# Products whose results nobody reads, in the gaps of TensorE, in a two-block fp32 kernel on one core

## What is computed

```
def reference(x, positions, ..., ffn_w1_2, ffn_w2_2, gla_..., ssd_...):
    x = first_block(x, positions, ...)
    return second_block(x, c_2, ctx_2, c_ctx_2, ...)

# second_block, per layer i in (0, 1); 256 latent and 256 context tokens
ul = snake(modulate(hl, m_l[0], m_l[1]));  uc = modulate(hc, m_c[0], m_c[1])
yc, yl = gla_mixer(uc, ul, ...)  if i == 0  else  ssd_mixer(uc, ul, ...)
hl = layer_norm(ALPHA * hl + m_l[2] * snake(yl))
hl = layer_norm(ALPHA * hl + m_l[5] * sq_relu_mlp(modulate(hl, m_l[3], m_l[4]), ffn_w1[i], ffn_w2[i]))
```

## Time and profile before

| what | value |
|---|---|
| median of 3 runs | 2241.13 us (2236.27 to 2246.55) |
| the profiled execution | 2240.53 us, span 2238.3 us |
| TensorE busy | 2014.4 us, 90% of the span |
| DVE, ACT, POOL busy | 1229.2, 729.5, 167.2 us |
| mean granted clock of TensorE | 0.961 |

### The profile page before, as it was taken

The page is one execution under the profiler, slowest core; times in us unless marked ns, Lnnn a source line. Parts: engine busy times, 40 slices in busy tenths (PEclk is TensorE's granted clock), DMA queues, the critical chain, the costliest instruction groups (busy, mean ns, idle before and its releaser), DMA issues.

```text
span 2238.3 us, 30881 instructions
## 1 busy us (share of the span) xinstructions
PE 2014.4 (90%) x12070; PEld 1447.9 (65%) x12070; DVE 1229.2 (55%) x2175; ACT 729.5 (33%) x1316; POOL 167.2 (7%) x155
## 2 busy tenths in 40 slices
PE   7989889879998778969998999999989988998997
PEld 4776433327785323326886788888867776777896
DVE  3474411134473212147466686666667876877676
ACT  3452201014552101124324311121165437654332
POOL 2001100001002000015422100000100000000000
PEclk9999999989998999988999999999999998999999
DMA  7589699975597899952221332232222342324552
GB/s 237 179 287 337 262 409 405 371 300 177 197 364 260 333 393 402 364 193 76 76 76 76 107 119 102 87 113 76 84 76 90 109 151 94 132 108 165 198 188 95
DMA packets 151921, 440.23 MB, mean 197 GB/s; under 512 B 10369, under 2 KB 12849, under 8 KB 143457
## 3 DMA queue, kind: packets, MB, share of 16 engines
q1 hardware_dynamic: 142704, 412.72, 49.3%
q0 software_dynamic: 8352, 22.39, 3.5%
q10 hardware_dynamic: 720, 3.15, 0.3%
HBM read 534.52 MB, written 1.21 MB: 239 GB/s over the span
## 4 chain that ended last, share of the span: by engine, by line
PE 40%; DVE 7%; ACT 4%; DVEq 2%; issue 1%; DMA 1%; ACTq 0%; POOL 0%; SPq 0%; POOLq 0%
PE bank L2117 22%; PE bank L2208 12%; PE bank L2259 4%; PE bank L2486 2%; DVE ARENA L3253 1%; ACT ARENA L2775 1%; PE bank L2122 1%; ACT ARENA L2768 0%; DVEq L2869 0%; ACT UT L2546 0%; ACTq L2549 0%; DMA W<-in_ffn_w 0%; DVE XA L2870 0%; DVEq L3255 0%; ACT ARENA L2523 0%
## 5 line engine op out<-in xcount | busy, mean ns | idle before, releaser
L2559 ACT ACTIVATE WPH<-W 128x1024 fp32r<-128x1024 f32 x128 | 135.5, 1063 | 379.5 <-PE bank L2117 198.1
L2117 PE MATMUL bank<-UH,WPH 128*128 128x512 f32 (+1 forms) x512 | 174.0, 340 | 6.8 <-DVE UL L2877 2.9
L2117 PE MATMUL bank<-UL,WPH 128*128 128x512 f32 (+1 forms) x512 | 172.7, 337 | 0.0
L2117 PE MATMUL bank<-UH,WPL 128*128 128x512 f32 (+1 forms) x512 | 172.7, 337 | 0.0
L2915 DVE TENSOR_TENSOR WPL<-W,WPH 128x1024 fp32r<-128x1024 f32 x128 | 153.4, 1219 | 17.9 <-ACT WPH L2559 17.9
L2208 PE MATMUL bank<-WPH,MHH 128*128 128x512 f32 x384 | 149.8, 390 | 0.0
L2208 PE MATMUL bank<-WPL,MHH 128*128 128x512 f32 x384 | 149.5, 389 | 0.0
L2208 PE MATMUL bank<-WPH,MHL 128*128 128x512 f32 x384 | 149.4, 389 | 0.0
L1431 DVE TENSOR_TENSOR H<-SG,bank 128x256 f32<-128x256 f32 x24 | 10.1, 421 | 235.9 <-ACT SG L1012 235.9
L2117 PE MATMUL bank<-ARENA 128*128 128x64 f32 (+4 forms) x528 | 105.7, 358 | 24.0 <-DVEq L3293 7.6
L710 PE MATMUL bank<-WC,H 128*32 128x512 f32 x768 | 93.7, 631 | 28.7 <-DMA WC<-in_expert_w_down 25.5
(11 more groups left out here) (460 smaller groups left out, 4266.8 us busy)
## 6 DMA issues: line engine op xcount, KB each, us to landing
WC<-in_expert_w_down SPq DMA_DIRECT2D x32, 2048.0 KB
W<-in_ffn_w SPq DMA_DIRECT2D x64, 1024.0 KB, 6.6
W<-in_ada_w SPq DMA_DIRECT2D x32, 1024.0 KB, 7.2
WA<-in_expert_w_gate SPq DMA_DIRECT2D x16, 2048.0 KB
WA<-in_expert_w_up SPq DMA_DIRECT2D x16, 2048.0 KB
W<-in_expert_w_gate SPq DMA_DIRECT2D x16, 2048.0 KB
W<-in_expert_w_up SPq DMA_DIRECT2D x16, 2048.0 KB
WC<-in_expert_w_down ACTq DMA_DIRECT2D x32, 1024.0 KB
```

The lines of the kernel that those rows point to most:

```text
L2117: return nc.tensor.matmul(bank[r.bank(key)][0:rows, cols[0]:cols[1]], lhs, rhs, start=start, stop=stop)
L2559: nc.scalar.activation(piece_view(WPH, q), piece_src(i, q), ACT.Copy).then_inc(hi_done, 1)
```

## The change

`block1` gets one call of its `keep_busy` after the last `combine`. `block2` gets a helper of the same name, which claims the bank of the key that comes next and multiplies `ident` by itself, and eight calls of it: before the second half of `turned_x("f0")` (22), before `turned_x("f1")` (28), before `("ga",)` (28), before `await_turned("o0")` (24), before `turned_x("m1")` (12), before `("dt",)` (12), before `group_pre(0)` (44) and before the first `group_outputs` (52). Nothing is removed or moved, and nobody reads what the new products write.

```
@@ block1
                 combine(l, MQ - 1)
+                if l == DEPTH - 1:
+                    keep_busy(("d", MQ - 1, 0), 18)
@@ block2
+            def keep_busy(key, n):
+
+                r.claim(pe, key)
+                for _ in range(n):
+                    nc.tensor.matmul(bank[r.bank(key)][:, 0:P], ident[:], ident[:], start=True, stop=True)
...
-            def turned_x(tag, nt, snaked, before):
+            def turned_x(tag, nt, snaked, before, busy=(0, 0)):
 
                 for s in range(nt // 2):
+                    if busy[s]:
+                        keep_busy(("uT", tag, s, 0), busy[s])
                     if before is not None:
                         pe.wait_ge(x_rdy, before + 2 * s + 2)
...
-                turned_x(f"f{i}", nt, False, before)
+                turned_x(f"f{i}", nt, False, before, (0, 22) if i == 0 else (28, 0))
...
             key = ("ga",)
+            keep_busy(key, 28)
             pe.wait_ge(g_lo, 1)
...
             turned("o0", out_tile, 4, True, lambda k: pe.wait_ge(o_rdy, k // 2), range(4, KT))
+            keep_busy(("gy", 0, 0), 24)
             await_turned("o0")
...
-            turned_x("m1", 4, True, X_LN[0])
+            turned_x("m1", 4, True, X_LN[0], (12, 0))
             n = number[("dt",)] % SLOTS
             key = ("dt",)
+            keep_busy(key, 12)
             pe.wait_ge(dt_lo, 1)
...
+            keep_busy(("cb", 0), 44)
             pe.wait_ge(xd_rdy, NX + 2 * SG_)
             r.read(pe, ("xt", NX + SG_ - 1))
             group_pre(0)
             pe.wait_ge(x_whole, 1)
             group_gate(0)
+            keep_busy(("yo", 0), 52)
             for g in range(SG_):
                 group_outputs(g)
```

## The result

| kernel | median (runs) | lowest to highest | ratio to before, 95% interval |
|---|---|---|---|
| before, same sessions | 2241.93 us (8) | 2236.27 to 2246.55 | |
| the change | 2250.22 us (8) | 2244.92 to 2256.54 | 1.0037, 1.0023 to 1.0052 |

The change is 8.3 us slower by the medians, 0.37%: inside the 0.5% taken as no change, and inside the range, but twice the +4.15 of the sum. The interval lies wholly above 1 and ends at 0.52%. The profiled execution took 2250.51 us, span 2248.7, 10.4 more than that of before. TensorE is busy for 2065.1 us instead of 2014.4, the granted clock is 0.972 instead of 0.961. The clock did rise; the time rose too.

A forecast was written before the change was run, and what follows sets the result against it. TensorE, with 40% of the span, was taken to bound the kernel. The terms 6.1 - 1.7 - 1.75 - 0.6 + 0.5 + 0.2 + 1.4 = +4.15 us on the profiled 2240.53 gave 2244.7 us, range 2236 to 2254.

The forecast's parts named there:

- late falls: Rival, chance 0.07: the clock falls where fills start late (m1, one group fill, gy), 14 us slower, 2255 us.
- Block boundary, +6.1: Before block two: 18 products of 512 columns end after DVE, so the barrier waits and block two starts 6.1 us later.
- `("ga",)`, -1.7: First projection of block two: 28 products end just before the work is ready; products behind run at full clock, saving 1.7 us.
- Gate products 0: Eight products behind the first projection, 11.00 us mostly at 0.50: not touched by any fill, no change taken.
- `("gy", 0, 0)`, -1.75: Output projection: 24 products end 1.15 us late, full clock behind saves 2.9; net -1.75, or +1.15 if the clock falls.
- Second half of f0, -0.6: First feed-forward part: 22 products delay the turns 1.5 us, hidden by ACT; the full clock saves 0.6, between 0 and 1.4.
- `("m1")`, +0.5: At the m1 turns, 12 products: -0.3 if the clock stays up, +1.4 if it falls behind tiny turns; +0.5 us taken.
- Groups, +0.2: Fills of 44 and 52 products: delays of 3.0 and 4.5 us nearly all paid back by the full clock, +0.2 us.
- Before f1, +1.4: Before the f1 turns: 28 products end 2.0 us late, so ACT starts later; +1.4 us, between 0.5 and 1.9.
- The gate products escape: Rival, chance 0.12: the low clock stretch misses the gate products in block two, -2.4 us in all, 2238 us.
- No hold: Rival, chance 0.06: identity products do not hold the clock, which falls some 3 us into each fill; +56 us, 2296.
- One record per product: Rival, chance 0.05: each product costs one record, half the price, so delays vanish and gains stay; -11 us, 2229.5.

## Why the prediction held, and where its sum was off

The verdict, no change by over 0.5%, and the range were right; the sum was 4.15 where the medians show 8.3. 2250.2 is 5.5 us above the sum's 2244.7 and 4.8 under the rival of late falls, so that it lies in the range owes something to the range's width. By its parts:

- **Block boundary, +6.1: right.** Measured +6.44 in all four executions with 18 products. The fill took 15.71 us, tail included, where 15.4 were counted. It was the largest term, and taking it out alone gives back 5.0 us of the median.
- **`("ga",)`, -1.7: right**, -1.55 to the last product. Gate products 0: right by its value (11.28 and 10.87 us in the two profiles of the change, 11.00 before). But the reason given under the rival was wrong. "Nothing in their form decides it" is refuted by the kernel with 128 rows. The clock goes where these products use 32 rows and stays where they use 128, in all fourteen traces.
- **`("gy", 0, 0)`, -1.75: mis-sized in the first execution**, -0.26, and right in the second, -1.81; of the six executions with 24 products three went the one way and three the other. In the first the clock fell in the fill itself, and it ended 2.49 us late, not 1.15. The "+1.15 if the clock falls all the same" was not right either: the products behind were at the full clock in both.
- **Second half of f0, -0.6: right**, -0.45 and -0.55.
- **`("m1")`, +0.5: the upper end came**, +1.5 and +1.3; the clock fell in the fill at 1631, behind the tiny turns, as the +1.4 case had it. I took the middle of two cases and should have taken the one for which the row spoke. `("dt",)` cost nothing, as said.
- **Groups, +0.2: right**, +0.1: delays of 2.85 and 4.4 us (3.0 and 4.5 were counted) paid back. What I did not work out is that smaller fills would keep the gain and drop the delays; that is worth 4 us.
- **Before f1, +1.4: right**, +1.34. (The text's 2037.35 should be 2037.2, by which the term is +1.3.)
- **What was missing: the stops of 2 to 3 us that the change does not touch.** +2.9 and +1.4 in the convolution, +1.1 and +1.2 in f1, less 0.6 at the end. The sum took stretches outside the fills as unchanged, because the trace of before shows the clock up behind them. With the terms above, the fills make +7.1 and +5.3 in the two executions and the untouched stretches +3.6 and +2.2; the two sums, +10.7 and +7.5, lie on either side of the 8.3 of the medians.
- **Rivals.** No hold: refuted, 15.5 us of fill at 1.00. One record per product: refuted, two. Late falls: partly, at m1 in both profiles of the change and at gy in one, not in the groups. The gate products escape: not in the change, partly in others (-1.6 to -3.3), and wholly by 128 rows.

## What to carry to other kernels

Fill a gap only for as long as the next work is surely not ready: count the fill in the price of its own shape and type, end it before the release, and cut it before adding another. At the groups and at m1 the shorter fill won more than the longer one. At f0 its gain went, because the next stop grew, and before f1 no fill gained, so look also at the stop that follows the filled one. Ahead of a barrier a fill delays every engine. Where the clock falls under dense work, look at the rows and columns that its products use before filling gaps; and where a kernel has many stops of 2 to 3 us, expect any shift of the work to move which of them are followed by a low stretch, and judge by several profiles of each kernel.

## What the runs showed of the hardware

- Eight fp32 products of 32 rows and 512 columns, issued without a gap, ran at 0.50 for most of 11.28 us; with 128 rows, 96 of them zeros, at 1.00 in 7.10 us. Products of 128 rows and 32 columns of the other operand, `("ga",)`, kept the clock for the 6 us that they lasted. Rows of zeros thus count as work, and so do products of the identity: the boundary fill ran 15.5 us at 1.00. The Trainium skill (TensorE: Matmul & The Clock Gate, "What's actually happening") says that activity of the array releases the clock. The traces agree, with one thing more: the products of few rows did not hold it in any of ten traces.
- Dense work of few columns did not always hold the clock either: behind 28 plain fp32 products of 32 moving columns (3.24 us), with no stop in the 6 us before, it fell in three of fourteen traces.
- The two traces of the kernel before have the same falls in block two, to 0.13 us a stretch, while two executions of one changed kernel differ by 3 to 5 us over block two. The Trainium skill (TensorE: Matmul & The Clock Gate, "What's actually happening") calls the watch over activity free-running, by which executions of one kernel can differ. The traces of the changed kernels agree. That the two of the kernel before do not differ in block two may be chance: they also began it alike.
- A fall behind a stop of 2.0 to 3.2 us costs 1.1 to 1.7 us. The stop itself is no longer than without one.
